# Folding and splitting the output weights inside the latent projection and the short group's attention

## The reference, cut to what matters

```
h = rmsnorm(x) * (1 + sc1) + sh1
z = h @ w_in
c_q, c_kv, k_pe, u = split(z)
att  = latent_attention(c_q, c_kv, k_pe, q_norm_g, kv_norm_g, w_uq, w_ukv)   # 8 heads, 512 columns
pool = einsum('bsgc,gcd->bsgd', mean - u, w_pool) * pool_scale               # 4 groups of 128, 512 columns
x = x + g1 * (concatenate([att, pool]) @ w_out)                              # w_out is 1024 x 1024
h = rmsnorm(x) * (1 + sc2) + sh2
return x + g2 * expert_choice_ffn(h, w_router, w_gate, w_up, w_down)
```

## Time and profile before

| what | value |
|---|---|
| median of 3 runs | 3984.77 us (3983.8 to 3984.88) |
| profiled execution | 3989.51 us |
| its span, first to last instruction | 3987.7 us |
| mean granted TensorE clock | 0.945 |
| busy: PE, PEld, DVE, ACT, POOL | 3606.0, 3087.7, 2024.9, 1886.9, 1349.5 us |
| latent_proj, first transfer to the next stage's first | 491.76 to 705.30 us |
| attention g = 0, first transfer to the next stage's first | 1522.05 to 1758.55 us |
| output_weights, first transfer to the next stage's first | 1758.55 to 1783.29 us |

### The profile page before, as it was taken

One profiled execution on the slowest core, in us unless ns is written; L12 is line 12 of the kernel. 1 busy time (PEld: TensorE's weight loads), 2 busy tenths in 40 slices (PEclk: granted clock), 3 DMA queues, 4 the chain that ended last, 5 costly groups with the idle time before them and its releaser, 6 DMA issues. The chain is left out here.

```text
span 3987.7 us, 53934 instructions
## 1 busy us (share of the span) xinstructions
PE 3606.0 (90%) x18897; PEld 3087.7 (77%) x18897; DVE 2024.9 (51%) x3120; ACT 1886.9 (47%) x3250; POOL 1349.5 (34%) x1008
## 2 busy tenths in 40 slices
PE   8799888699999997969994699999999999999991
PEld 1799866577777775747773599999999999999991
DVE  0333254688888885852225644444444444444433
ACT  0444232588888895852331234444344443444333
POOL 0212057688988897862221000000000000000000
PEclk9799989799999998989995799999999999999995
DMA  7422299422222205325651355444444445554437
GB/s 254 137 104 97 95 363 367 112 43 43 43 44 43 43 6 110 66 73 181 183 175 67 108 157 158 146 149 152 144 147 148 151 152 158 158 154 145 153 101 274
DMA packets 350654, 538.90 MB, mean 135 GB/s; under 512 B 33926, under 2 KB 234886, under 8 KB 347530
## 3 DMA queue, kind: packets, MB, share of 16 engines
q1 hardware_dynamic: 326476, 448.61, 35.9%
q0 software_dynamic: 13824, 50.34, 5.2%
q10 hardware_dynamic: 10176, 37.75, 2.4%
HBM read 394.08 MB, written 142.46 MB: 135 GB/s over the span
## 5 line engine op out<-in xcount | busy, mean ns | idle before, releaser
L1230 POOL TENSOR_TENSOR att_pr<-att_e,att_pr 128x512 fp32r<-128x512 f32 x640 | 813.4, 1294 | 144.0 <-ACT att_pr L1117 133.2
L1994 POOL DMA_INDIRECT s_x<-moe_ye,moe_to_add x48 | 90.9, 1893 | 1436.3 <-DVE moe_ye L2185 1426.6
L1161 DVE TENSOR_REDUCE att_mx<-att_m_ps 128x1 f32<-128x512 f32 x640 | 423.7, 682 | 111.5 <-PE att_m_ps L1022 101.8
L2130 DVE TENSOR_TENSOR keep_wl<-keep_raw,keep_wh 128x1024 fp32r<-128x1024 f32 x380 | 440.0, 1221 | 33.6 <-ACT keep_wh L2083 33.6
L2083 ACT ACTIVATE keep_wh<-keep_raw 128x1024 fp32r<-128x1024 f32 x380 | 370.0, 1045 | 126.1 <-PE moe_d_ps L2060 126.1
L1063 PE MATMUL att_o_ps<-att_pr,att_v 128*128 128x512 f32 x1280 | 408.2, 400 | 4.7 <-POOL att_pr L1230 4.6
L1117 ACT ACTIVATE att_pr<-att_e 128x512 fp32r<-128x512 f32 x640 | 402.8, 629 | 18.5 <-issue 2.8
L1111 ACT ACTIVATE att_e<-att_s_ps 128x512 f32<-128x512 f32 x640 | 379.6, 593 | 64.2 <-PE att_s_ps L1051 18.0
L1183 DVE TENSOR_TENSOR att_acc_ps<-att_acc_ps,att_e 128x512 f32<-128x512 f32 x544 | 375.1, 690 | 17.2 <-ACT att_e L1111 11.4
L2110 ACT ACTIVATE moe_silu<-moe_a_ps 128x384 f32<-128x384 f32 x128 | 63.0, 492 | 645.1 <-PE moe_u_ps L2033 645.1
L2031 PE MATMUL moe_a_ps<-moe_xh,keep_wh 128*128 128x384 f32 x1024 | 345.4, 337 | 2.1 <-DVE moe_xl L2138 2.1
(11 more groups left out here) (268 smaller groups left out, 7695.3 us busy)
## 6 DMA issues: line engine op xcount, KB each, us to landing
keep_raw<-w_gate SPq DMA_DIRECT2D x64, 1024.0 KB, 5.3
keep_raw<-w_up SPq DMA_DIRECT2D x64, 1024.0 KB, 7.8
keep_raw<-w_down SPq DMA_DIRECT2D x64, 1024.0 KB, 6.3
ada_wa<-w_ada SPq DMA_DIRECT2D x12, 2048.0 KB, 10.2
s_ct<-inp_ct SPq DMA_DIRECT2D x24, 640.0 KB, 3.0
prj_ct<-s_ct SPq DMA_DIRECT2D x6, 2560.0 KB, 16.3
s_kn<-prj_out SPq DMA_DIRECT2D x24, 512.0 KB, 12.3
s_qn<-prj_out SPq DMA_DIRECT2D x24, 512.0 KB, 12.4
```

What stands on the lines that cost most here:

```text
L1161: nc.vector.tensor_reduce(mx[:, u % CB, u // CB:u // CB + 1], m_ps[u % MB][:, :], AX, ALU.max).then_inc(max_part, 1)
L1230: nc.gpsimd.tensor_tensor(pr[:, s % RING, 1, :], e[:, s % RING, :], pr[:, s % RING, 0, :].bitcast(F32), ALU.subtract).then_inc(lo_done, 1)
L2130: nc.vector.tensor_tensor(wl[:, s, part, :], raw[:, s, part, :], wh[:, s, part, :].bitcast(F32), ALU.subtract).then_inc(w_lo_done, 1)
```

## The change

`output_weights` is deleted, and its work goes to two places.

In `latent_proj`, SP loads `w_pool`, `pool_scale` and two row blocks of the lower half of `w_out` after block 0. In block 1 one extra product `w` turns `w_pool`, and ScalarE copies it with the scale (the scale moves from `w_out` to `w_pool`; GpSimd has no part in it). In block 2 eight extra products `f` (128x512 each), two after every `v`, form the folded weights; ScalarE copies each, and SP stores it to a new scratch tensor `s_wo`. The two remaining row blocks are loaded in between. Since the positions 5 and 10 count the extra entries too, `store_diff` and `fetch` move ahead by a few products in blocks 1 and 2.

In `attention` of g = 0, iteration 0 only, the weights (upper half from `w_out`, lower half from `s_wo`) are loaded in row blocks of 512 KB into a ring of two and split in 16 pieces of 128x512: ScalarE's part after `exps(s)` at steps s with s % 4 = 1, VectorE's part after `add_up(s - 1)` at s % 4 = 3. `wo_h` and `wo_l` are allocated ahead of this attention.

```diff
+    FOLD_BLOCK = 2
+    for b in range(NB):
+        folds = 0
+        for kind, i in ORDER:
+            OPS.append((b, kind, i))
+            if b == FOLD_BLOCK - 1 and (kind, i) == ("v", 0):
+                OPS.append((b, "w", 0))
+            if b == FOLD_BLOCK and kind == "v":
+                OPS += [(b, "f", folds + j) for j in range(2)]
+                folds += 2
...
+            def load_wo(g):
+                sp.dma_start(kvraw[:, g % 2, :], w["w_out"][0][HEADS * VD + g * P:HEADS * VD + (g + 1) * P, :]
+                             ).then_inc(wo_in[g % 2], 16)
...
+                elif kind == "f":
+                    g, c = i // 2, i % 2
+                    sp.wait_ge(fold_done, i + 1)
+                    sp.dma_start(w["s_wo"][g * P:(g + 1) * P, c * BANK:(c + 1) * BANK],
+                                 fold[:, c * BANK:(c + 1) * BANK]).then_inc(fold_stored[c], 16)
+                    if c == 1 and g + 2 < len(WINDOWS):
+                        load_wo(g + 2)
...
+                if q + 1 == ENDS[b]:
+                    if b == 0:
+                        sp.wait_ge(w_lo_done, ALL_PIECES)
+                        sp.dma_start(wp.rearrange("p (g d) -> p g d", d=P), w["w_pool"][0].rearrange("g c d -> c g d")
+                                     ).then_inc(wp_in, 16)
+                        sp.dma_start(scale[:, :], w["pool_scale"][0].rearrange("(g p) -> p g", p=P),
+                                     allow_slow_non_contiguous=True).then_inc(wp_in, 16)
+                        for g in range(2):
+                            load_wo(g)
+                    if b + 2 < NB:
+                        sp.wait_ge(ready, ENDS[b])
+                        load(b + 2)
...
         def _(pe):
...
+                if kind == "f":
+                    g, c = i // 2, i % 2
+                    if i == 0:
+                        pe.wait_ge(wpt_done, len(WINDOWS))
+                    pe.wait_ge(wo_in[g % 2], 16 * (g // 2 + 1))
+                    nc.tensor.matmul(dst, wpt[:, g * P:(g + 1) * P], kvraw[:, g % 2, c * BANK:(c + 1) * BANK],
+                                     start=True, stop=True).then_inc(ready, 1)
...
         def _(act):
...
+                if kind == "f":
+                    if i >= 2:
+                        act.wait_ge(fold_stored[i % 2], 16 * (i // 2))
+                    nc.scalar.activation(fold[:, i % 2 * BANK:(i % 2 + 1) * BANK], src, ACT.Copy).then_inc(fold_done, 1)
...
 def attention(nc, w, keep, g):
...
+        def weight_piece(it, s, first):
+            if g == 0 and isinstance(it, int) and it == 0 and s % 4 == first:
+                n = s // 4
+                part = slice(n % 2 * BANK, (n % 2 + 1) * BANK)
+                return n, wraw[:, n // 2 % 2, part], keep["wo_h"][:, n // 2, part], keep["wo_l"][:, n // 2, part]
...
                 load_qk(i, i)
                 load_v(i, i)
+            if g == 0:
+                for n in range(2):
+                    load_wo(n)
...
                     if from_start(it, b - 1):
                         store(it, b - 1)
                         fold(it, b - 1)
                         store_inverses(it, b - 1)
+                    if g == 0 and it == 0 and 1 <= b < KD - 1:
+                        sp.wait_ge(wo_lo_done, 2 * b)
+                        load_wo(b + 1)
...
         def _(act):
...
                     exps(it, s)
+                    piece = weight_piece(it, s, 1)
+                    if piece:
+                        n, src, hi, _ = piece
+                        act.wait_ge(wo_in[n // 2 % 2], 16 * (n // 4 + 1))
+                        nc.scalar.activation(hi, src, ACT.Copy).then_inc(wo_hi_done, 1)
...
         def _(dve):
...
                         add_up(it, s - 1)
+                    piece = weight_piece(it, s, 3)
+                    if piece:
+                        n, src, hi, lo = piece
+                        dve.wait_ge(wo_hi_done, n + 1)
+                        nc.vector.tensor_tensor(lo, src, hi.bitcast(F32), ALU.subtract).then_inc(wo_lo_done, 1)
...
-def output_weights(nc, w, keep):
...
-                output_weights(nc, w, keep)
```

More of the change, by code:

```diff
@@ L553, in latent_proj @@
         ends = m.sb("ends", [P, 2 * PAD])
+        scale = m.sb("scale", [P, len(WINDOWS)])
+        spare = qraw[:].rearrange("p k n -> p (k n)")
+        wp, wpt, fold = (spare[:, i * BANK:(i + n) * BANK] for i, n in ((0, 1), (1, 1), (2, 2)))
         ps = [m.ps(f"ps{i}") for i in range(BANKS)]
@@ new lines, in _ @@
+            for q, (b, kind, i) in enumerate(OPS):
+                at = q - (ENDS[b - 1] if b else 0)
+                if at in (PER // 3, 2 * PER // 3):
+                    n = 2 * b + int(at > PER // 2)
+                    store_diff(n)
+                    if n + 2 < len(JOBS):
+                        fetch(n + 2)
+                slot = SLOT.get(kind, 0) + i
+                if kind == "r":
+                    sp.wait_ge(rope_lo_done, count_before(q + 1, "r"))
+                elif kind == "f":
[5 more added lines that the diff above has]
+                        load_wo(g + 2)
+                elif kind in "kqv":
+                    sp.wait_ge(lo_done, count_before(q + 1, "kqv"))
+                if kind in "rkqv":
+                    src = out[:, slot].bitcast(F32)
@@ L735, in _ @@
+            for c in range(2):
+                sp.wait_ge(fold_stored[c], 16 * len(WINDOWS))
             for slot in range(SLOTS):
@@ new lines, in _ @@
+                slot = SLOT.get(kind, 0) + i
+                src = ps[q % BANKS][:, :]
+                if kind in "wf":
+                    continue
+                if kind in "rt":
+                    rope = count_before(q + 1, "r")
+                    dve.wait_ge(ready, q + 1)
+                    if kind == "r" and rope > 1:
+                        dve.wait_ge(qf_done, rope - 1)
+                    table = cos if kind == "r" else sin
+                    nc.vector.tensor_tensor(prod[:, int(kind == "t"), :], src, table[:, t0:t0 + BANK],
+                                            ALU.mult).then_inc(prod_done, 1)
+                    if kind == "t":
+                        if rope > 1:
+                            dve.wait_ge(rope_lo_done, rope - 1)
+                        dve.wait_ge(prod_done, 2 * rope)
+                        nc.vector.tensor_tensor(qf[:, :], prod[:, 0, :], prod[:, 1, :], ALU.add).then_inc(qf_done, 1)
+                        dve.wait_ge(rope_hi_done, rope)
+                        hi, lo = (out[:, SLOT["r"] + i, l, :] for l in range(2))
+                        nc.vector.tensor_tensor(lo, qf[:, :], hi.bitcast(F32), ALU.subtract).then_inc(rope_lo_done, 1)
+                    continue
@@ L2285, in build @@
         latent_proj(nc, w, keep)
-        for g in (1, 0):
-            attention(nc, w, keep, g)
+        attention(nc, w, keep, 1)
+        out_ctx = ctx.enter_context(ExitStack())
+        tile(out_ctx, "wo_h", [P, KD, D], F32R, side="right")
+        tile(out_ctx, "wo_l", [P, KD, D], F32R, side="right")
+        attention(nc, w, keep, 0)
         with ExitStack() as route_ctx:
             tile(route_ctx, "logits", [P, TOKENS])
-            with ExitStack() as out_ctx:
-                tile(out_ctx, "wo_h", [P, KD, D], F32R)
-                tile(out_ctx, "wo_l", [P, KD, D], F32R)
-                output_weights(nc, w, keep)
-                out_proj(nc, w, keep)
+            out_proj(nc, w, keep)
+            out_ctx.close()
             tile(moe_ctx, "raw", [P, 2, KD, BANK], side="right")
@@ L2321 @@
     "s_diff": [DP // P, P, TOKENS],
+    "s_wo": [DP, D],
     "s_x": [TOKENS, D],
```

284 lines of the change are left out of this document (97 added, 187 removed).

## The result

| | before | after |
|---|---|---|
| median of 4 runs | 3984.28 us (3979.98 to 3984.88) | 4052.44 us (4051.78 to 4053.48) |
| ratio | | 1.0176, 95% interval 1.0163 to 1.019 |
| profiled execution, its span | 3989.51, 3987.7 us | 4051.78, 4050.0 us |
| latent_proj, first transfer to the next stage's | 213.5 us | 492.38 to 714.60 = 222.2 us |
| attention g = 1, the same way | 816.75 us | 812.88 us |

The change makes the kernel 1.8% slower by the ratio above; the medians are 68.2 us apart. By stage: -24.7 + 8.7 + 72.1 + 8.7 = +64.8 us. Attention g = 1, whose code is the same, was 3.9 us shorter in this execution (in the traces of the experiments it takes 812.6 to 818.6 us); together with smaller differences that makes the 62.3 us between the two spans. A stage's time from one trace is therefore good to a few us only.

The account below looks back on a forecast made before the run. Bound: the DMA engines in latent_proj; in attention g = 0 VectorE's list and the two hand-overs after it. -24.7 + 12.0 + 17.5 + 0.6 + 51 = +56.4 us on 3984.8 gives 4041 us, range 4010 to 4060.

Parts of the forecast that it names:

- the rival of larger stalls: Attention g = 0: load takes 6.2 us, TensorE stays at 1.2 GHz; 10.65 us per stall, 4054 us; chance 0.18.
- The stage that goes: output_weights removed, out_proj starting directly behind attention: -24.7 us, bounds 24 to 26.
- The fold: latent_proj: 4.46 MB more in a full DMA queue delay job 10 and the end, +12.0 us (8 to 15).
- The waits in its chain: latent_proj: ScalarE's waits for stores and TensorE's for row blocks, charged 0, up to 3 us kept.
- The first wait: Attention g = 0, block 0, step 1: ScalarE's first piece waits for load_wo(0), +17.5 us (13.5 to 18.5).
- Block 1: Attention g = 0: VectorE's piece at step 3 adds 0.6 us; the other pieces fit the pauses.
- Six stalls: Attention g = 0, blocks 2 to 7: load_wo(m) issued too late, 8.5 us per block, 51 us (31.5 to 64).
- The third piece of the term: Attention g = 0, blocks 2 to 7: net 0.45 us per block beyond the wait (-0.6 to +1.3), including TensorE's low clock.
- VectorE's pieces in blocks 2 to 7: Attention g = 0: pieces at step 3 fall where the stall has emptied VectorE, 0 us.
- `out_proj`, no term at all: out_proj: only its earlier start was counted; no cost of its own was charged.
- The rival that the pieces land in time: Attention g = 0: only VectorE's step-3 pieces count, 4.8 us; total -7.9, 3977 us; chance 0.04.
- The rule that decides it: Attention g = 0: whether load_wo(m) has landed when exps(8m + 1) ends decides if pieces land in time.

Follow-up runs that it names:

- experiment 4: The kernel before with the changed latent_proj; output_weights kept, s_wo written and not read: 3993.88 us, ratio 1.003.
- experiment 7: experiment 2 with VectorE's pieces at steps 7 and 0 of the next block, and four places for folded pieces instead of two: 3984.61 us, ratio 1.0007.
- experiment 2: Experiment 1 with load_wo(0) and load_wo(1) behind the first head's loads, ahead of the other heads': 3989.47 us, ratio 1.0019.
- experiment 6: experiment 2 with GpSimd's subtraction on 32 of 512 columns in steps 16 to 63 of the short group's first iteration: 3986.65 us, one run.
- Experiment 1: The changed kernel with load_wo(b + 1) and its wait ahead of everything else of block b in SP's list: 4006.81 us, ratio 1.0061.
- experiment 3: The kernel before with wo_h and wo_l allocated from the right end of SBUF, nothing else: 3989.08 us, ratio 1.0019.
- experiment 10: The kernel before with 32 bytes left free ahead of the expert stage's tiles on the right side of SBUF: 3989.6 us, one run.
- experiment 11: experiment 8 with 96 bytes left free instead of 32, so wo_h starts at a multiple of 128: 3983.61 us, one run.
- experiment 8: experiment 3 with 32 bytes left free ahead of the output weights, so wo_h starts at a multiple of 64: 3986.73 us, ratio 1.0018.

## Why the prediction came out as it did

The direction and the main mechanism, a load issued behind a wait, were right. 4052 us lies in the range, 11 us above the forecast of 4041. That it is close to the rival of larger stalls (4054) is luck: a stall came to 9.55 us, not that rival's 10.65, and 7 to 9 us come from a stage that no term of the sum covers. Step by step:

- *The stage that goes, -24.7.* As forecast: the next stage begins behind attention with nothing in between.
- *The fold, +12.0 (8 to 15).* 11.4 us by experiment 4's medians; 8.7 by the two traces, 13.2 by the means of five and six. The size fits the bytes. The waits in its chain, charged at nothing with up to 3 in the bounds, did open a hole (share 0.21 and 0.19). With the hole closed the stage is 3 us shorter in the mean of three traces, and the time of experiment 7 did not move: whether the 0 should have been 1 to 3 stays open.
- *The first wait, +17.5 (13.5 to 18.5).* ScalarE waited 15.82 us and block 0 grew by 15.4. Experiment 2 took 14.5 us of it away by the place of the load alone.
- *Block 1, +0.6.* It was 1.36. The mis-sized step is one VectorE instruction taken at the mean of its list (0.53 us): it takes 1.44 us here in the trace after, beside GpSimd, and 0.68 without it (experiments 2 and 6). ScalarE's copies, taken at 0.52 in the same way, last 0.62.
- *Six stalls, +51.* They were 57.3: 9.55 each for 8.5. The delay of the issue was 3.17 us (3.15 said), the landing 5.3 in the mean (4.9 said); the waits are 50.8 in sum, or 8.47 each, for 8.05. The third piece of the term was too small: I gave TensorE 3 to 4 us at the low clock and 0.45 us net, and it runs 5 to 6 us at 0.50 and the blocks grow by 1.1 us beyond the wait. How much of the 1.1 is the clock and how much the pieces no run separates. Experiment 1 confirms the cause. The waits are longer in blocks 2, 4 and 6 (8.5 to 9.6) than in 3, 5 and 7 (7.8 to 8.1); in the former SyncE issues a head's q, k and v right behind the row block, which lands after 5.3 to 6.4 us there and 4.7 to 5.0 in the others.
- *VectorE's pieces in blocks 2 to 7, 0.* About right for this kernel, as the stall had emptied VectorE (the step-3 piece lasts 0.77 to 0.79 us behind a stall). It was cover, not absence: with the stall gone they cost 1.6 us a block (experiments 1 and 2).
- *`out_proj`, no term at all.* This step failed, by 8.7 us in the trace and 7.1 in experiment 3's (6.6 by its medians). I looked at what the stage waits for and not at where its operand now lies. "Allocated ahead of this attention" stood in the diff with `side="right"`, and I read it as free.

Of the 11.8 us between the forecast change (56.4) and the measured one (68.2), `out_proj` has 7 to 9, the stalls 6.3 and block 1 0.8; the first wait gives back 2.1 and the fold, by experiment 4, 0.6. The rest is within what single traces differ by. So errors of both signs cancelled in part.

The rival that the pieces land in time was worth 3977 by my sum, and the chip's version of it (experiment 2) is 3989.5. The rule that decides it, whether `load_wo(m)` has landed when `exps(8m + 1)` ends, was the right one, but what it gives was 12 us too good: the pieces cost some 11 us in the eight blocks and not 4.8, and `out_proj` about 7.

## What to carry to other kernels

A transfer that is queued behind a wait in an engine's ordered list is as late as that wait, however idle the queues are. Ask for each load what stands ahead of it and when that is released, and for each short transfer on a closed cycle what is put ahead of it. When a stall goes, look again at every cost that it hid: here one instruction on VectorE had to move to a place where it idled, and one transfer by a few lines, before the folded version won 0.4% instead of losing 1.8%. And an allocation is a part of a change: compare the spacing of the matmuls that read a tile before and after it has been moved, in every use of the tile and over many rows: four rows of experiment 10 look the same as before's, five thousand don't.

## What the runs showed that I had not expected

- A matmul of `out_proj` takes 0.2276 to 0.2278 us with the moving operand at a multiple of 128 bytes, on either side of SBUF, 0.2293 at a multiple of 64, and 0.2335 at 32 past one, all at a clock of 1.00 (the kernel before and experiments 11, 8 and 3). The expert stage's down projection repeats the last two: 0.2335 at 32 past one and 0.2297 at a multiple of 64 (experiment 10, one run).
- In the same run the matmuls that have these tiles as the stationary operand went the other way: 0.1735 us at 32 past a multiple of 64, 0.1756 at a multiple of 64. Why stays open.
- VectorE's subtraction with both inputs in SBUF takes 0.68 us alone and 1.32 to 1.73 at step 3, beside GpSimd's. GpSimd's four take 5.48 us instead of 5.05. VectorE's 128x512 operations that read PSUM last 0.68 to 0.69 us in the mean of the same stretch (experiment 2).
- After 8 us of waiting TensorE was granted 1.2 GHz for 6 us, and was busy for 5.85 of them.
- A transfer of 2 KB that lands in 2.0 us on a quiet queue needed 4.4 to 4.9 behind a head's q, k and v (1.8 MB), and 6.0 to 6.4 with a row block of 0.5 MB among them.
